# Moving the gate expansion of a dense expert stage to earlier steps, with a smaller candidate list in the top-16 selection

## The reference, cut to what matters

```python
s = jnp.einsum('thpd,hpkd->thpk', q, keys)            # 8 heads, 2 halves, 128 keys each
sv, si = lax.top_k(s, 16)                             # the best 16 of each half
cand = sv[:, :, 0, :, None] + sv[:, :, 1, None, :]    # 16 x 16 sums
cv, ci = lax.top_k(cand.reshape(N, 8, 256), 16)       # the best 16 of 256
i1 = take_along_axis(si[:, :, 0], ci // 16); i2 = take_along_axis(si[:, :, 1], ci % 16)
eidx = i1 * 128 + i2                                  # 128 experts of each token
gate = softmax(cv)
h = gelu(u_tab[eidx] . x)                             # then out = sum of gate * h * v_tab[eidx]
```

## Time and profile before

| what | value |
| --- | --- |
| median of three runs | 2313.19 us (2308.82 to 2318.27) |
| profiled execution, its own time | 2299.57 us |
| its span, first to last instruction | 2297.8 us |
| PE busy in the span | 1972.6 us (86%) |
| DVE busy | 1512.0 us (66%) |
| ACT busy | 891.1 us (39%) |
| POOL busy | 784.5 us (34%) |
| mean granted TensorE clock | 0.946 of full |
| bytes moved | 513.02 MB, mean 223 GB/s |

### The profile page before, as it was taken

The page is one execution under the profiler, slowest core; times in us unless marked ns, Lnnn a source line. Parts: engine busy times, 40 slices in busy tenths (PEclk is TensorE's granted clock), DMA queues, the critical chain, the costliest instruction groups (busy, mean ns, idle before and its releaser), DMA issues. The chain is left out here.

```text
span 2297.8 us, 29795 instructions
## 1 busy us (share of the span) xinstructions
PE 1972.6 (86%) x11493; PEld 1785.1 (78%) x11493; DVE 1512.0 (66%) x2468; ACT 891.1 (39%) x1752; POOL 784.5 (34%) x440
## 2 busy tenths in 40 slices
PE   4999479848898898899899998777756999998998
PEld 3998479738797697799899997666645888777876
DVE  3676444271323212492799896999966888988888
ACT  2455112111422113333444343777753334433434
POOL 0233123012531023276576776333321222222221
PEclk9999689869999999999999998999988999999999
DMA  4221100022453313256699997789889999999996
GB/s 125 65 74 40 44 1 1 5 83 83 129 202 101 129 39 114 64 173 229 250 335 337 328 328 284 270 317 346 332 345 343 397 401 402 394 401 378 396 401 244
DMA packets 211501, 513.02 MB, mean 223 GB/s; under 512 B 13216, under 2 KB 143008, under 8 KB 174496
## 3 DMA queue, kind: packets, MB, share of 16 engines
q1 hardware_dynamic: 183712, 309.77, 39.0%
q0 software_dynamic: 27648, 201.34, 22.2%
HBM read 451.26 MB, written 59.80 MB: 222 GB/s over the span
## 5 line engine op out<-in xcount | busy, mean ns | idle before, releaser
L1557 POOL TENSOR_TENSOR ex_ulo<-ex_u,ex_uhi 128x1024 fp32r<-128x1024 f32 x128 | 324.5, 2540 | 312.8 <-ACT ex_uhi L1588 310.4
L1671 PE MATMUL ps<-xhi,ex_uhi 128*128 128x384 f32 x1024 | 356.0, 348 | 24.3 <-POOL ex_ulo L1557 18.7
L1671 PE MATMUL ps<-xhi,ex_ulo 128*128 128x384 f32 x1024 | 346.3, 338 | 0.0
L1671 PE MATMUL ps<-xlo,ex_uhi 128*128 128x384 f32 x1024 | 346.3, 338 | 0.0
L1951 PE MATMUL ps<-po_vhi,po_whi 128*128 128x512 f32 x768 | 239.4, 393 | 49.9 <-DVE po_wlo L1985 49.2
L1295 POOL DMA_INDIRECT ga_ring<-in_uv,ga_idx x138 | 171.7, 1244 | 292.0 <-DVE po_acc_s L1321 175.3
L1918 ACT CAST po_vhi<-po_v 128x1024 fp32r<-128x1024 f32 x128 | 133.8, 1047 | 327.7 <-DMA po_v<-in_peer_v 291.7
L1951 PE MATMUL ps<-po_vlo,po_whi 128*128 128x512 f32 x768 | 238.5, 392 | 0.0
L1951 PE MATMUL ps<-po_vhi,po_wlo 128*128 128x512 f32 x768 | 237.7, 391 | 0.0
L1671 PEld LDWEIGHTS ps<-xhi,ex_uhi 128*128 128x128 f32 x1024 | 195.4, 191 | 29.0 <-POOL ex_ulo L1557 22.7
L1951 PEld LDWEIGHTS ps<-po_vhi,po_whi 128*128 128x128 f32 x768 | 143.8, 189 | 84.0 <-issue 54.0
(11 more groups left out here) (379 smaller groups left out, 4205.4 us busy)
## 6 DMA issues: line engine op xcount, KB each, us to landing
ex_u<-in_uT SPq DMA_DIRECT2D x128, 512.0 KB, 5.6
po_v<-in_peer_v SPq DMA_DIRECT2D x64, 1024.0 KB, 10.4
acts<-ex_h SPq DMA_DIRECT2D x64, 384.0 KB, 3.0
gates<-scores SPq DMA_DIRECT2D x12, 2048.0 KB, 7.3
po_w<-acts SPq DMA_DIRECT2D x32, 768.0 KB, 12.7
po_g<-gates SPq DMA_DIRECT2D x32, 768.0 KB, 15.8
in_w_raw<-in_w_in SPq DMA_DIRECT2D x24, 512.0 KB, 4.0
at_cache<-in_cacheT SPq DMA_DIRECT2D x6, 1024.0 KB, 5.8
```

Source lines behind the costliest of these rows:

```text
L1557: pool.tensor_tensor(ulo[:, j % 3], u[:, j % 3], uhi[:, j % 3].bitcast(F32), ALU.subtract).then_inc(low, 1)
L1671: mm = pe.matmul(ps[:, j % 2, 0:ND], w[:, j % 3, k, :], x[:, k, :], start=(k == 0 and n == 0), stop=(k == KT - 1 and n == 2))
```

## The change

It has these parts.

- The 16 x 16 sums are replaced by 65: the pair (a, b) of the sorted halves can be among the best 16 only where (a+1)(b+1) is small enough. Five additions of 16, 16, 16, 16 and 1 sums fill a row of 72 slots per head. From the place of a chosen sum the two ranks are decoded by integer operations (shifts, masks, a power of two made in the exponent).
- FIRST_SPREAD goes from 104 to 85, with three quads a step instead of four (PER_STEP = 3), over 32 steps up to 116; one pick goes with three quads.
- The early picks are weighed at steps 20 + 4n//3, the gates' exp is in step 19, the first seven gathers are at step 13. Picks 46 and 47 come after the last selection. Twenty late picks (LATE) follow in steps 117 to 126, two a step. LOOP_PICKS becomes 100, of which all and four more are fetched in this block (before: 96 and seven more).
- The exp of the dense tokens' gates moves to step FIRST_SPREAD - 2.
- The one-hots are in three buffers instead of two, ACT scales the second in place, and does so two quads ahead instead of one.
- SP's writes of `gates` stand at the step in which the eighth quad of a group falls, now also at odd steps.

```diff
-FIRST_SPREAD = 104
+FIRST_SPREAD = 85
+PER_STEP = 3
 QUADS = ND // 4
 EARLY = 48
-LOOP_PICKS = EARLY + 2 * (NKEY - FIRST_SPREAD)
+LATE = 20
+LOOP_PICKS = EARLY + QUADS // PER_STEP + LATE
+SLOTS = 72
+def pick_step(n):
+    if n < EARLY - 2:
+        return 20 + 4 * n // 3
+    if n < EARLY:
+        return FIRST_SPREAD - 1
+    if n < LOOP_PICKS - LATE:
+        return FIRST_SPREAD + n - EARLY
+    return FIRST_SPREAD + QUADS // PER_STEP + (n - LOOP_PICKS + LATE) // 2
...
 # SP
-                g = (j - FIRST_SPREAD) // 2 - 1
-                if g >= 0 and j % 2 == 0:
-                    sp.wait_ge(spread_out, NG_QUADS * (g + 1))
+                for g in range(ND // 32):
+                    if j == FIRST_SPREAD + NG_QUADS * (g + 1) // PER_STEP:
+                        sp.wait_ge(spread_out, NG_QUADS * (g + 1))
...
 # POOL
-            for n in range(LOOP_PICKS + gather.SLOTS):
+            for n in range(LOOP_PICKS + 4):
                 before = n - gather.SLOTS
...
+                step = 13 if before < 0 else pick_step(min(before + 2, LOOP_PICKS - 1)) + 1
...
 # ACT
+                if j == FIRST_SPREAD:
                     scale(0)
+                    scale(1)
+                for x in range(PER_STEP):
+                    q = PER_STEP * (j - FIRST_SPREAD) + x
+                    if 0 < q <= QUADS:
+                        evict(q - 1)
+                    if 0 <= q < QUADS - 2:
+                        scale(q + 2)
                 for n in at.get(j, []):
                     gather.weigh(act, n)
...
 # DVE, selection
-                after(dve.tensor_tensor(cand[:, 0:nh, :].rearrange("p h (a b) -> p h a b", a=TOPK),
+                dve.memset(cand[:, 0:nh, 65:SLOTS], LOWEST)
+                for a0, na, nb, c0 in ((0, 1, 16, 0), (1, 2, 8, 16), (3, 4, 4, 32), (7, 8, 2, 48), (15, 1, 1, 64)):
+                    ins = dve.tensor_tensor(cand[:, 0:nh, c0:c0 + na * nb].rearrange("p h (a b) -> p h a b", a=na),
...
+                dve.tensor_scalar(c3[:, 0], flat, TOPK - 1, TOPK, ALU.bitwise_and, ALU.bitwise_or)
+                after(dve.tensor_scalar(c3[:, 1], flat, 4, None, ALU.logical_shift_right))
+                dve.tensor_scalar(p2[:, 0], c3[:, 1], 127, None, ALU.add)
+                after(dve.tensor_scalar(p2[:, 1], c3[:, 1], -1.0, 127.0, ALU.mult, ALU.add))
+                after(dve.tensor_scalar(p2, p2, 23, None, ALU.logical_shift_left))
+                after(dve.tensor_tensor(c3[:, 2], c3[:, 0], p2[:, 0].bitcast(F32), ALU.mult))
...
 # DVE, quads
-                if q >= 2:
-                    dve.wait_ge(spread_mm, q - 1)
+                if q >= 3:
+                    dve.wait_ge(spread_mm, q - 2)
...
-                if q % 2:
-                    pick(EARLY + q // 2)
+                if q % PER_STEP == PER_STEP - 1:
+                    pick(EARLY + q // PER_STEP)
+            for n in range(LOOP_PICKS - LATE, LOOP_PICKS):
+                pick(n)
```

More of the change, by code:

```diff
@@ L1508, in peer_experts @@
         spread = [s_flat[:, i * 32 * P:(i + 1) * 32 * P].rearrange("p (e t) -> p e t", t=32) for i in range(2)]
[L1509 to L1512, removed]
+        l_flat = lookup[:, :, :].rearrange("p a j -> p (a j)")
+        cand = l_flat[:, 0:PH * SLOTS].rearrange("p (h c) -> p h c", h=PH)
+        quads = [l_flat[:, 0:1024], l_flat[:, 1024:2048], s_flat[:, 64 * P:72 * P]]
+        hot = [x.rearrange("p (i t k) -> p i t k", i=2, t=4) for x in quads]
         u_loaded = [sem(f"ex_u_loaded{i}") for i in range(3)]
@@ L1591, in scale @@
                 act.wait_ge(hots, q + 1)
-                if q >= 2:
-                    act.wait_ge(spread_mm, q - 1)
                 for t in range(4):
-                    ins = act.activation(hot2g[:, q % 2, t], hot2[:, q % 2, t], ACT.Copy,
+                    ins = act.activation(hot[q % 3][:, 1, t], hot[q % 3][:, 1, t], ACT.Copy,
                                          scale=pickT[:, 2, 4 * q + t:4 * q + t + 1])
@@ L1608, in _ @@
             at = {}
-            for n in range(EARLY):
-                at.setdefault(early_step(n), []).append(n)
+            for n in range(LOOP_PICKS):
+                at.setdefault(pick_step(n), []).append(n)
             first(0)
@@ L1622, in _ @@
                     first(j + 2)
-                if j == early_step(0):
+                if j == pick_step(0) - 1:
                     act.wait_ge(dropped, 1)
                     act.activation(gather.gate[:, :], gather.gate[:, :], ACT.Exp).then_inc(exps, 1)
-                if j == FIRST_SPREAD:
+                if j == FIRST_SPREAD - 2:
                     act.wait_ge(dropped, 2)
                     act.activation(drops[:, :], drops[:, :], ACT.Exp).then_inc(exps, 1)
+                if j == FIRST_SPREAD:
                     scale(0)
+                    scale(1)
[5 more added lines that the diff above has]
+                        scale(q + 2)
                 for n in at.get(j, []):
                     gather.weigh(act, n)
[L1632 to L1642, removed]
         @block.tensor
@@ L1650, in quad @@
                 for t in range(4):
[L1651 removed]
+                    mm = pe.matmul(ps[:, 2 + q % 2, t * P:(t + 1) * P], hot[q % 3][:, 0, t], hot[q % 3][:, 1, t],
                                    start=True, stop=True)
@@ L1674, in _ @@
                         mm.then_inc(products, 1)
-                    if k % 2 and j >= FIRST_SPREAD:
-                        quad(4 * (j - FIRST_SPREAD) + k // 2)
+                    x = PER_STEP * (j - FIRST_SPREAD) + k // 2
+                    if k in (1, 3, 5) and 0 <= x < QUADS:
+                        quad(x)
         @block.vector
@@ L1785, in between @@
                     norm_gates(g, NPICK // TOPK, g, 1)
-                for x in range(2):
-                    pick(16 * t + 2 * i + x)
+                if t < DT - 1 or i < 7:
+                    for x in range(2):
+                        pick(16 * t + 2 * i + x)
             for t in range(DT):
@@ L1799, in _ @@
                               ALU.mult).then_inc(gated, 1)
+            for n in range(EARLY - 2, EARLY):
+                pick(n)
             for t in range(DT):
@@ L1896, in _ @@
         def _(pool):
-            for n in range(LOOP_PICKS + gather.SLOTS, NPICK):
+            for n in range(LOOP_PICKS + 4, NPICK):
                 gather.fetch(pool, io, n)
```

48 lines of the change are left out of this document (21 added, 27 removed).

## The result

The changed kernel takes 2378.49 us (median of four runs, 2372.07 to 2385.70) beside 2311.01 us of the kernel before: the ratio is 1.0294, 95% interval 1.0246 to 1.0342. It is slower by 3%, where 1% faster was forecast; 2378 lies above the range's 2316, and above the 2334 of the slowest rival. The profiled execution has a span of 2370.3 us instead of 2297.8.

A forecast was written before the change was run, and what follows sets the result against it. PE bounds the early steps with transfers close behind, DVE the expansion. Gains of 10.5 + 13.5 - 3 + 3 = 24 us take 2313.2 to 2289 us; range 2258 to 2316.

The forecast's parts named there:

- the slowest rival: Expansion: SP's queue starves ACT for good, loads behind the gates landing in 13.5 instead of 8.2; 2334 us, chance 0.12.
- the part on the expansion: 32 steps from step 85: DVE needs 7.9 us a step, SP's late loads make it 8.2, in all 262 us.
- The absorption: Expansion: DVE runs two quads ahead during ACT's waits, so ACT's own time decides; T = 8.1, taken as 8.2.
- the formula: Expansion pitch T: ACT's 6.7 us plus load lateness 11.9 - T in twelve of 32 steps; gives 8.1.
- the "0.9 before" of the prediction: Expansion of the kernel before: the load behind the gates' write landed 0.9 us before ACT's cast wanted it.
- Steps 21 to 84: Stretch before the expansion: denser gathers raise the pitch to 4.42 us; step 85 begins near 1347.
- The sign that the prediction named: Steps 21 to 84: if the cast waits often there, the prediction is wrong and transfers are to blame.
- Ready in time: DVE is ready for first gathers at step 13, exp at step 19 and, with 13 us to spare, step 83.
- The turn: Passage into the expansion: cost 11.7 us before, now 7 us (4 to 10).
- From gelu 116 on: Late picks, steps 117 to 127: nine steps of 7.5 us, one 4.7, one 4.2; 76 us (66 to 88).
- The selection: DVE's selections: 7.7 us less for a full one, half for the half one, 35 us of DVE time in all.
- The end of the block: Last gelu to next block's first load: 23.0 us becomes 9.5, 13.5 gained; three more gathers cost 3, given back.

The follow-up runs named there:

- The late wait alone, in the kernel before: Kernel before, with SP waiting for two evicts more ahead of each write of gates but the last: 2392.44 us, ratio 1.0354.
- The slower pace: Kernel with the load of ex_u ahead of the gates' write, early picks at 3/2 instead of 4/3 steps (40 early, 24 late): 2298.50 us, ratio 0.9929.
- the try to show it alone, on the kernel before: Kernel before, with ACT's cast behind the four quads of its step from step 104 on: 2421.91 us, ratio 1.0500.

## Why the prediction was wrong, step by step

- **The failed step** is in the part on the expansion: "DVE can run two quads ahead meanwhile, so I let ACT's own time decide: T = 6.7 + 12/32 x (11.9 - T)". The place, the cause and the order (SP's wait ahead of the load, cast, `evict`, DVE) were right. The absorption was not. It needs DVE to be far ahead, and DVE, which sets the pitch, is not: it made one quad more and waited 10.28. What fits is the plain pitch plus the whole wait: 8.2 + 67.1/32 = 10.3, measured 10.2. The late wait alone, in the kernel before, shows it without the rest of the change. One such wait stood already in the trace of before, and the prediction did not use it. ACT's timeline before, gelus 112 and 113:

```profile
1533.68 0.47 ACT L1619 ACTIVATE ex_h<-ps 128x384 f32<-128x384 f32 x1
...
1536.99 1.04 ACT L1588 CAST ex_uhi<-ex_u 128x1024 fp32r<-128x1024 f32 x1 [2.84 <-DMA ex_u<-in_uT]
...
1548.14 0.47 ACT L1619 ACTIVATE ex_h<-ps 128x384 f32<-128x384 f32 x1
```

  The step has 14.5 us instead of 11.4, so 2.8 us of waiting made it 3.0 longer.
- The wait itself was 6.0 us on average (66.2 behind the eleven writes in the expansion) where the formula gave 3.7 at T = 8.2. SP was released at 1.9, 3.6 and 6.65 to 7.3 us for the first, second and third quad (forecast 1.9, 3.6, 5.3; ACT's own wait for DVE came on top). From the load's issue to the start of the waiting cast it was 8.3 to 11.6 us, 10.0 in the mean, not 8.2: I took the minimum of the earlier trace rows where its median of 10.4 stood beside it. With the median and no absorption, at the forecast pitch of 7.9, a step is 7.9 + 12/32 x (14.1 - 7.9) = 10.2, the expansion 327 us, and the sum 2354.
- Even where SP was released no later than before, at 1.9, the cast waited 2 to 3 us: a plain step is 3.2 us shorter than it was, and the cast wants its load that much sooner. The formula has this in its T; the "0.9 before" of the prediction does not follow from its own terms, which give 11.8 - (1.9 + 0.3 + 8.2) = 1.4.
- The rival that SP's queue starves ACT, with 2334, had the direction right, but not for its reason: it wanted loads that land in more than 11.3 us in the mean.
- **Steps 21 to 84**: forecast 4.42 a step, measured 4.70 (300.8 us for 64), 18 us more. (Up to gelu 20 it was 6 us less than forecast, as the burst of the first gathers cost 7 us there and not 13.) The slower pace shows that the density of the gathers is the cause of these 18. My own bound, 1.51 MB at the 324 GB/s of the earlier trace rows, was 4.66. The 395 GB/s of another block was no argument for this one. The profile after has 310 GB/s here at a share of 0.84. Why the mixture stops there was not found. The sign that the prediction named, a cast that waits often here, tells nothing by its count: 36 waits in this stretch, and 42 in the same one of before.
- **Ready in time**: right. The first exp waited for nothing but ACT's order (DVE idle 10.6 us before it, forecast 20), and the dense selections were over before ACT's exp of step 83: DVE waited 13.4 us for it, forecast 13.
- **The turn**: 7.4 us, forecast 7. **Plain pitch**: 8.13 to 8.33, forecast 7.9; the held one-hot took 2.8 instead of 2.5, near the bound of a full lock that the prediction gave. **From gelu 116 on**: 76.6, forecast 76. DVE waits for gathers there, 31.9 us, as forecast, but the steps range from 5.3 to 11.6 us where an even 7.5 was forecast, so the exact sum is in part luck.
- **The selection**: forecast 35 us less for DVE, 22 measured. The small integer instructions take 0.22 us alone, but some met POOL; the groups of DVE from 1059 to 1350 us, after:

```profile
L1744 DVE FIND_INDEX8 ex_topi<-ex_top,ex_lookup 128x8 uint32<-128x72 f32 x24 | 4.9, 228 | 0.0
...
L1757 DVE TENSOR_SCALAR ex_code<-ex_code 128x128 uint32<-128x128 uint32 x3 | 6.1, 2040 | 0.1
...
L1758 DVE TENSOR_SCALAR ex_code<-ex_code 128x128 uint32<-128x128 uint32 x3 | 0.6, 216 | 0.0
```

  The searches on 72 elements cost 228 ns, as worked out. Of a shift and a mask of the same size the shift took 2040 ns on average and the mask, next in line, 216. By the timeline the three shifts took 0.23, 2.78 and 3.11 us; the two long ones began 0.3 and 0.6 us before a subtraction of POOL's and ended with it.
- **The end of the block**: 13.5 us gained by forecast, 9.3 by the profile, and the first product of the next block came 7.5 us later after its first load, where I had taken 3, with nothing given back. The kernel with seven gathers ahead shows these as the same bytes: what one side of the meeting loses the other gains.
- The sum by the profile, from gelu 0: +24.1 us in the first 84 steps (forecast +12), +42.9 in the rest (-23), -9.3 at the end (-13.5), +7.2 behind it (0), together +65 against -24.

## What to carry to other kernels

Before a wait is put into a queue that also loads, work out when the instruction behind it is wanted; here writes released up to 5.3 us later than they used to be, in steps 3.2 us shorter, cost 3% of the kernel, and letting the next load go first gave it back. A wait on an engine with idle time is not absorbed if the engine that sets the pitch needs something that stands behind it; look for who has a lead, not for who has slack. Take the transfer rate for a stage from that stage's own mixture.

## What the runs showed of the hardware that was not expected

- The time of a repeated loop depends on where POOL's subtraction falls among DVE's instructions: the same instructions gave a pitch of 8.13 us, and of 7.5 with the cast moved behind the quads among ACT's instructions of a step. This is read from the two traces; the try to show it alone, on the kernel before, ran into late gathers.
- A small instruction can pay as much as a large one: a shift on 128 elements took 2.78 and 3.11 us where POOL's subtraction fell on it, and 0.23 where it did not; the one-hot of 512 elements took 2.78 instead of 0.6.
- In the step with the stall of 8.70 us the granted clock of PE was 0.69 in the mean, and the first quad took 2.04 us, where a quad takes 1.05 otherwise; quads took 1.05 again within the same step. The step was 8.45 us longer than a plain one, with 8.70 of waiting, so nothing that the clock cost shows in its length; it was not measured apart.
